# A gate tile behind each query tile, in a PSUM bank of its own, in the second attention block

## The reference

```python
for i in range(DEPTH):
    h = rmsnorm(x, norm_g[i])
    mem_h = rmsnorm(mem, mem_norm_g[i])
    ...
    else:
        proj = jnp.einsum('bsd,de->bse', h, w_in_b[j])
        o_mix = mixer_axial_gqa(proj[..., :c1], proj[..., c1:c2], proj[..., c2:c3], qn_b[j], kn_b[j], ang_b)
        q_mem = proj[..., c3:c4]
        gate = proj[..., c4:]
    o_mem = memory_attention(q_mem, mem_h, w_mem_kv[i], mem_qn_g[i], mem_kn_g[i])
    y = jnp.concatenate([o_mix, o_mem], axis=-1) * jax.nn.silu(gate)
    x = x + jnp.einsum('bse,ed->bsd', y, w_out[i])
```

## Time and profile before

| | |
|---|---|
| median of 3 runs (lowest, highest) | 3470.26 us (3469.72, 3470.77) |
| the profiled execution's own time | 3469.21 us |
| its span, first to last instruction | 3467.4 us |
| PE busy | 3342.7 us, 96% of the span |
| ACT, DVE, POOL busy | 1365.4, 1408.3, 1476.0 us |
| mean granted TensorE clock | 0.987 |

### The profile page before, as it was taken

The page is one execution under the profiler, slowest core; times in us unless marked ns, Lnnn a source line. Parts: engine busy times, 40 slices in busy tenths (PEclk is TensorE's granted clock), DMA queues, the critical chain, the costliest instruction groups (busy, mean ns, idle before and its releaser), DMA issues.

```text
span 3467.4 us, 45465 instructions
## 1 busy us (share of the span) xinstructions
PE 3342.7 (96%) x16418; PEld 2766.5 (80%) x16418; DVE 1408.3 (41%) x2428; ACT 1365.4 (39%) x2184; POOL 1476.0 (43%) x1111
## 2 busy tenths in 40 slices
PE   8999999899999999999988999988999999999998
PEld 7888876788888888887777888877888888887777
DVE  2221455552214622044465322174365266244533
ACT  3222435542224522232554322266355255454543
POOL 5544433055543555434312554435454354353322
PEclk9999999999999999999999999999999999999999
DMA  4222212022222222222201222222221222231111
GB/s 156 97 97 97 86 61 67 1 86 96 97 97 85 88 96 96 97 80 85 67 25 49 95 96 94 97 101 91 79 74 63 74 78 67 76 125 66 55 51 61
DMA packets 76758, 281.70 MB, mean 81 GB/s; under 512 B 8512, under 2 KB 8640, under 8 KB 76224
## 3 DMA queue, kind: packets, MB, share of 16 engines
q1 hardware_dynamic: 75600, 274.66, 23.7%
q10 hardware_dynamic: 1008, 4.98, 0.4%
HBM read 277.51 MB, written 2.10 MB: 81 GB/s over the span
## 4 chain that ended last, share of the span: by engine, by line
PE 88%; DVE 6%; ACT 3%; issue 2%; POOL 0%; DVEq 0%; ACTq 0%; POOLq 0%
PE ps L1869 16%; PE ps L1871 16%; PE ps L1870 16%; PE ps L1941 4%; PE ps L1943 4%; PE ps L1942 4%; PE ps L2398 2%; PE ps L2412 2%; PE ps L1978 2%; PE ps L1980 2%; PE ps L1979 2%; PE ps L2337 1%; PE ps L2339 1%; PE ps L2338 1%; PE ps L2381 1%
## 5 line engine op out<-in xcount | busy, mean ns | idle before, releaser
L565 POOL TENSOR_TENSOR w_lo<-raw,w_hi 128x512 fp32r<-128x512 f32 x1028 | 1379.6, 1365 | 1712.8 <-ACT w_hi L631 1712.8
L1869 PE MATMUL ps<-x_hi,w_hi 128*128 128x512 f32 x2560 | 1022.6, 399 | 1.1 <-DVE b_q L1665 1.0
L1871 PE MATMUL ps<-x_hi,w_lo 128*128 128x512 f32 x2560 | 997.9, 390 | 0.0
L1870 PE MATMUL ps<-x_lo,w_hi 128*128 128x512 f32 x2560 | 997.4, 390 | 0.0
L631 ACT ACTIVATE w_hi<-raw 128x1024 fp32r<-128x1024 f32 x514 | 541.2, 1055 | 1001.4 <-PE ps L1871 522.4
L1869 PEld LDWEIGHTS ps<-x_hi,w_hi 128*128 128x128 f32 x2560 | 481.7, 188 | 109.4 <-issue 9.7
L1870 PEld LDWEIGHTS ps<-x_lo,w_hi 128*128 128x128 f32 x2560 | 481.7, 188 | 105.4 <-issue 8.6
L1871 PEld LDWEIGHTS ps<-x_hi,w_lo 128*128 128x128 f32 x2560 | 481.1, 188 | 101.9
L1274 DVE TENSOR_TENSOR T<-T,ps 128x512 f32<-128x512 f32 x66 | 45.3, 687 | 496.6 <-PE ps L1871 490.2
L585 POOL TENSOR_TENSOR square_parts<-T,square_parts 128x512 fp32r<-128x512 f32 (+1 forms) x71 | 87.5, 1234 | 255.0 <-ACT square_parts L977 255.0
L1978 PE MATMUL ps<-h_hi,w_hi 128*128 128x512 f32 (+1 forms) x440 | 153.2, 348 | 0.0
(11 more groups left out here) (331 smaller groups left out, 5123.8 us busy)
## 6 DMA issues: line engine op xcount, KB each, us to landing
raw<-in_weights SPq DMA_DIRECT2D x514, 512.0 KB, 3.3
Y<-in_x_t SPq DMA_DIRECT2D x1, 2048.0 KB, 8.0
mem<-in_mem_t ACTq DMA_DIRECT2D x2, 1024.0 KB, 7.1
out_t<-Y SPq DMA_DIRECT2D x8, 256.0 KB, 2.2
ple_p<-in_p_t ACTq DMA_DIRECT2D x2, 512.0 KB, 5.5
mat<-in_mats SPq DMA_DIRECT2D x1, 768.0 KB, 11.7
masks<-in_masks ACTq DMA_DIRECT2D x1, 768.0 KB, 9.0
rope<-in_rope_a ACTq DMA_DIRECT2D x1, 512.0 KB, 9.9
```

The costliest lines, as they stand in the source:

```text
L565: ins = pool.tensor_tensor(g.wl[:, k, part], g.raw[:, k, part], g.wh[:, k, part], ALU.subtract)
L1869: mm(out, wh[:, c], xh[:, kc, :], start=kc == 0, stop=False)
L1870: mm(out, wh[:, c], xl[:, kc, :], start=False, stop=False)
L1871: ins = mm(out, wl[:, c], xh[:, kc, :], start=False, stop=kc == DC - 1)
```

## The change

The eight query tiles and the first eight gate tiles take turns. A query tile has a group in its middle only for t = 2, 4, 6; each has a group behind it. Then comes a gate tile with a group in its middle and one behind it. Gates 8 to 11 follow as before. Query tiles all use bank 0; the gates between them use bank 1, and gates 8 to 11 take banks 0 and 1 in turn. The waits on PE and ACT follow: a query tile waits until the one before it has been read by the rope, and a gate tile until the last gate in its bank has been copied. The weight stream is packed in the new order. No instruction is added or taken away.

```diff
--- before.py
+++ after.py
@@ -293,15 +293,23 @@
         ops += [Unit("b_k", u + t, t, R_B + t, groups.pop(0)), groups.pop(0), Sum(R_B + t, S)]
     for t in range(2):
         ops += [Unit("b_v", u + 2 + t, t, None, groups.pop(0)), groups.pop(0)]
-    for t in range(8):
-        mid = groups.pop(0) if t in (0, 3, 5, 7) else None
-        ops += [Unit("b_q", u + 4 + t, t, R_B + 2 + t, mid), groups.pop(0), Sum(R_B + 2 + t, S)]
+    u += 4
     for t in range(12):
-        mid = groups.pop(0) if groups else None
-        ops.append(Unit("gate", u + 12 + t, t, None, mid))
-        if groups:
-            ops.append(groups.pop(0))
+        if t < 8:
+            mid = groups.pop(0) if t in (2, 4, 6) else None
+            ops += [Unit("b_q", u, t, R_B + 2 + t, mid), groups.pop(0), Sum(R_B + 2 + t, S)]
+            u += 1
+        ops += [Unit("gate", u, t, None, groups.pop(0)), groups.pop(0)]
+        u += 1
     return ops + groups
+
+
+def raw_bank(r):
+    return r % 2 if r < R_B + 2 else 0
+
+
+def gate_bank(i, t):
+    return 1 if i and t < 8 else t % 2
 
 
 def between(ops):
@@ -962,7 +970,7 @@
     def qk_square(r, src, width=S):
         if roped(r):
             act.wait_ge(s.rope_read, r + 1 - (R_A if r < R_MEM[1] else R_A + 8))
-            src = ps[:, r % 2, :]
+            src = ps[:, raw_bank(r), :]
         else:
             act.wait_ge(s.qraw_done, r + 1)
         cols = square_cols(r, width)
@@ -1094,9 +1102,9 @@
                 hi(op.u + 4)
                 if op.kind == "gate":
                     act.wait_ge(s.unit_done, op.u + 1)
-                    if op.t == 0:
-                        act.wait_ge(s.qk_done, (R_MEM[1], R_B + 10)[i])
-                    fn(g.G[:, op.t, :], ps[:, op.t % 2, :], ACT.Copy).then_inc(s.gate_done, 1)
+                    if i == 0 and op.t == 0:
+                        act.wait_ge(s.qk_done, R_MEM[1])
+                    fn(g.G[:, op.t, :], ps[:, gate_bank(i, op.t), :], ACT.Copy).then_inc(s.gate_done, 1)
                     if i == 0 and op.t == GATES_BEFORE:
                         act.preload_act_table(ACT.Silu)
                         for t in range(EARLY):
@@ -1643,7 +1651,7 @@
 
     def qk_rope(r, u):
 
-        x, gain, raw = normed(g, r), qk_gain(r), ps[:, r % 2, :]
+        x, gain, raw = normed(g, r), qk_gain(r), ps[:, raw_bank(r), :]
         cos, sin = g.ROPE[:, 0, :], g.ROPE[:, 1, :]
         dve.wait_ge(s.consts_done, 7)
         dve.wait_ge(s.unit_done, u + 1)
@@ -2482,12 +2490,14 @@
                 value_unit(op.u, op.t, 4, 256, g.XH, g.XL, natural, range(4), op.mid, None,
                            R_B + 1 if op.t == 0 else None)
             elif op.kind == "gate":
-                pe.wait_ge(s.qraw_done, (R_MEM[1], R_B + 10)[i])
-                if op.t >= 2:
-                    pe.wait_ge(s.gate_done, 12 * i + op.t - 1)
-                tile(op.u, 0, ps[:, op.t % 2, :], g.XH, g.XL, op.mid)
+                bank = gate_bank(i, op.t)
+                pe.wait_ge(s.qraw_done, R_B + 2 + min(op.t, 8) if i else R_MEM[1])
+                last = [t for t in range(op.t) if gate_bank(i, t) == bank]
+                if last:
+                    pe.wait_ge(s.gate_done, 12 * i + last[-1] + 1)
+                tile(op.u, 0, ps[:, bank, :], g.XH, g.XL, op.mid)
             else:
-                pe.wait_ge(s.qraw_done, op.r - 1)
+                pe.wait_ge(s.qraw_done, op.r - (raw_bank(op.r) != raw_bank(op.r - 1)))
                 if op.kind == "b_q":
                     pe.wait_ge(s.vcopy_done, V_B + (4 if op.t else 1))
                 if op.kind == "a_qk":
@@ -2496,7 +2506,7 @@
                 if op.kind == "mem_k":
                     tile(op.u, 0, ps[:, op.r % 2, 0:N_MEM], g.MH, g.ML, op.mid)
                 else:
-                    tile(op.u, 0, ps[:, op.r % 2, :], g.XH, g.XL, op.mid)
+                    tile(op.u, 0, ps[:, raw_bank(op.r), :], g.XH, g.XL, op.mid)
 
     def tail(i):
         u0 = BASE["AB"][i] + (U_A, U_B)[i] - 12
@@ -2584,8 +2594,9 @@
     parts += [weight_tiles(w[:, qm + mem_w:]), weight_out(x["w_out_2"][0])]
     w = x["w_in_b_2"][0]
     parts += memory_units(kv[1], w[:, 1536:2048])
-    parts += [weight_tiles(w[:, 1024:1280]), weight_moving(w[:, 1280:1536], 256), weight_tiles(w[:, 0:1024]),
-              weight_tiles(w[:, 2048:]), weight_out(x["w_out_2"][1])]
+    q, gate = weight_tiles(w[:, 0:1024]), weight_tiles(w[:, 2048:])
+    parts += [weight_tiles(w[:, 1024:1280]), weight_moving(w[:, 1280:1536], 256)]
+    parts += [np.stack([q[:8], gate[:8]], axis=1).reshape(16, P, UNIT), gate[8:], weight_out(x["w_out_2"][1])]
     return np.concatenate(parts, axis=0)
```

## The result

The changed kernel takes 3480.72 us, median of 9 runs (3479.24 to 3482.34). The kernel before took 3469.72 beside it, median of 9 (3469.22 to 3471.13). The ratio is 1.0031, with a 95% interval of 1.0022 to 1.0040: **11.0 us slower**. The profiled execution of the changed kernel took 3481.58 us, with a span of 3479.8 us.

A forecast was written before the change was run, and what follows sets the result against it. TensorE was taken to bound the kernel, losing time only by idling or a lower clock. Query tiles +9.7 and the end +3.5 gave +13.2 us on 3469.21, so 3482.4, or 3483.4 on the median; range 3473.5 to 3490.

The forecast's parts named there:

- the side that held 0.85: Whole kernel: slower by over 0.2% (6.9 us), given 0.85.
- The cover rule: Query tiles: a query tile, a group, twelve matmuls and another group give a wait; a whole tile between gives none.
- the number of waits: Query and gate stretch: the waiting pattern eight times where it was four; waits 15.1 us after, 7.16 before.
- The moved scaling on DVE: Between rope and maximum: the scaling of the tile before goes away, saving nothing, as DVE had 0.8 us of slack.
- Rival 2: Behind query tiles DVE does bind: each of eight waits loses 0.6 us, -4.8, so 3478.6; chance 0.09.
- The banks and the gate's copy: Bank waits and ACT's copy of a gate tile: costed at nothing; without cover the copy would cost 4.8 us.
- The end: Behind the last gate tile: one group more left over, copy +2.36, clock 1.1, together +3.5 us.
- The clock: Behind the 2.61 and 2.33 us waits: two falls, 3.4 us, before one, 1.7; 1.1 at the end.
- The sign that was to show it: Changed kernel's query and gate stretch: granted clock about 0.66 behind two of the eight waits.
- 1 (the clock falls behind all eight): Query and gate stretch: clock falls behind all eight waits, six more falls, +10.2, so 3493.6; chance 0.08.
- 3 (waits only moved, 3473.8): Query tiles: a gate tile in front absorbs four of eight waits; only the end's +3.5 is paid, 3473.8; chance 0.08.
- 4 (the wait goes away): Gate tile's middle group: ACT reaches its copy before square's high part and cast; -5.4, so 3464.9; chance 0.05.

The follow-up runs named there:

- experiment 3: Changed kernel with the group in the middle of gates 0 to 7 behind 15 of the tile's matmuls, not 12: 3473.45 us, ratio 1.0009.
- (2): Changed kernel with the middle group of gates 0 to 7 moved into the query tile in front: 3475.2 us, ratio 1.0014.
- (1): Changed kernel with the cast of a weight unit issued on ACT behind the group that follows each query tile: 3470.43 us, ratio 1.0000.
- Experiment 8: Kernel before with the cast on ACT behind its eight query tiles issued behind the next group: 3465.48 us, ratio 0.9987.
- (4): Kernel before, order kept, with all query tiles in bank 0, each waiting for the one in front: 3478.01 us, ratio 1.0021.
- the second profile: Changed kernel, unchanged, profiled and timed again: 3481.03 us (6 runs), ratio 1.0031 to the kernel before.

## Why the prediction was right, and where it was off

The forecast was 3483.4 us, measured 3480.72, within the range and on the side that held 0.85. The 2.7 us between them are the clock, priced 2.8 too high. Two smaller errors cancel each other by luck: each wait was priced 0.16 us too low, 0.5 in all, and the kernel before took 0.5 us less beside the changed one (3469.72) than the 3470.26 that the forecast started from. Step by step:

- **The cover rule and the number of waits: right.** Eight, at 2.63, 2.35 and 1.69 us, sum 15.1 as forecast. Their price was a little low, since the idle time in a bracket was taken for the whole cost: 0.5 us for three waits more, as shown above. Both ends of the difference were tested. Three matmuls more of cover take 0.65 off each wait (experiment 3), a whole tile of it takes all away but 0.61 us (2), and 1.05 us less in the chain take 1.0 to 1.2 off each (1). So the cause is shown: the group in the gate's middle comes 12 matmuls behind one whose ACT part stands behind square and cast.
- **The moved scaling on DVE, costed at no gain: right.** Rival 2 (DVE binds, 3478.6) lies 2.1 us below the measured time and the forecast 2.7 above it, so the median alone would not have told them apart. The rows do: 1.69 and not 1.1 for each wait, and a chain of 6.27 us against 6.26. Experiment 8 shows where the slack of 0.8 us ends: with the cast away, DVE binds in the order of before.
- **The banks and the gate's copy, costed at nothing: right,** but only for this order. Alone the banks cost 7.5 us (4).
- **The end: right in the wait, off in its clock.** Forecast 2.36 and 1.1 for the clock. The 2.36 came as 2.44 with the clock up, and the fall cost 1.7 where it came.
- **The clock: this step failed.** "After: two falls, 3.4 us; before: one fall, 1.7 us": I priced a fall behind each wait of over 2.3 us of the query tiles, and a part of one more at the end. The runs show one fall in the three long waits of each execution, in the query stretch or at the end, and before one as well. So the clock adds nothing to the difference where I had 1.7 + 1.1 = 2.8 us. The sign that was to show it, 0.66 behind two of the eight waits, did not come: it stood behind none of them in the first profile and behind one in the second. The forecast's +13.2 less 2.8 is 10.4, and the 0.5 of the brackets makes 10.9; measured 11.0.
- **The rivals.** 1 (the clock falls behind all eight): none of the six waits of 1.69 us has a clock below 1.00 in the one profile, and over 3193 to 3350 us the mean is 1.00 and 0.99. What the Trainium skill, page "TensorE: Matmul & The Clock Gate", section "A second HAM failure mode: psum-queue depth-cycling", tells of another kernel, that frequent short idle times make the clock swing, did not happen behind these six. They came 20 to 22 us apart, not the 18 of the forecast; the one fall of the second profile stands behind the 2.35. 3 (waits only moved, 3473.8) falls with the eight waits. 4 (the wait goes away): the change did not do it, but its mechanism was the right lever. Its price was in part what experiment 1 paid back, 10.3 us.

What stays open is which of the long waits brings the clock down. Outside key tile 0, 16 waits of 2.3 to 2.65 us stand in the profiles of these kernels, and it fell behind six; the same wait of the same kernel had it in one execution and not in the next. It also fell behind both waits of 2.08 and 2.09 us of experiment 4, and behind none of the waits up to 1.96 us in the query and gate tiles. So the length alone does not decide between 2.08 and 2.65. Key tile 0's wait of 2.6 us brought it down to 0.66 in all ten profiles that have it, and at 1.5 us in none of three. What differs between the two places was not tried.

## What to carry to other kernels

In a software pipeline, count for each step the work that lies between it and the step that needs its result, after every change of order: here a pattern with a wait of mostly 1.69 us went from four places to eight, and that was the larger part of the loss. When such a wait stands, look first at what its chain queues behind on each engine, and ask of each instruction there who needs it now; one cast of 1.05 us behind each query tile, issued a group later, was worth 10.3 us in one order and 5.0 in the other (1.7 of each by the clock, going by the profiles), and the next engine's queue (DVE's scaling, then POOL's low part) bound right behind it. Count also what the new order leaves over at the end: each group without a tile beside it cost 2.3 us.

## What the runs showed of the hardware

The granted clock is not a fixed property of a place in a program. With the nine waits the same to 0.02 us, one profile of the changed kernel has 0.66 behind the wait of 2.35 us and 1.00 behind the end's 2.31, the other the reverse (0.56 at the end). In the kernels of these runs, a fall in the changed part costs 1.7 us, so a sum over single profiles carries an error of that size for each long wait. Medians of several runs even this out. The point in the program at which key tile 0's wait ends lay between 3163.20 and 3166.20 us in thirteen profiles, although the code ahead of it is the same in all (three of them end that wait 1.1 us sooner, since it is part of their edit). That is 3 us that a single span can be off, and the reason why the stretches were measured from there.
